# Hyena filter spectra from even and odd taps: half the transform matmuls on TensorE, sums and differences on VectorE

## What is computed

```
h = (sin-MLP of position features) -> (L, 2, n_ch); h = h * exp(-t * |deltas|)
h_full = concat([h[:, 0], zeros(1), h[1:, 1][::-1]]); h_full /= sum |h_full|
filt_f = rfft(h_full)                       # spectrum of each filter, for 2 orders
for n, gate in enumerate((x1, x2)):         # order o = 0, 1
    z = gate * (irfft(rfft(z, 2L) * filt_f[:, n])[:L] + bias[n] * z)
```

## Time and profile before

| | us |
|---|---|
| median of 3 runs (2746.61 to 2751.88) | 2748.93 |
| the profiled execution, whole | 2745.32 |
| its span in the trace | 2743.7 |
| PE busy | 2642.8 (96%) |
| DVE busy | 1875.4 (68%) |
| ACT busy | 1309.8 (48%) |

### The profile page before, as it was taken

One profiled execution on the slowest core, in us unless ns is written; L12 is line 12 of the kernel. 1 busy time (PEld: TensorE's weight loads), 2 busy tenths in 40 slices (PEclk: granted clock), 3 DMA queues, 4 the chain that ended last, 5 costly groups with the idle time before them and its releaser, 6 DMA issues.

```text
span 2743.7 us, 48997 instructions
## 1 busy us (share of the span) xinstructions
PE 2642.8 (96%) x17192; PEld 2341.7 (85%) x17192; DVE 1875.4 (68%) x3349; ACT 1309.8 (48%) x2366; POOL 111.9 (4%) x206
## 2 busy tenths in 40 slices
PE   7999999999999999999989999999999999999998
PEld 6889999888987778998779999988799877799986
DVE  7788787634567867566678778786255678765666
ACT  5555555534553333453455555555355433344535
POOL 2100000000000000000030000000000000000000
PEclk9999999999999999999999999999999999999999
DMA  7544444334453324555564444443444423345554
GB/s 244 163 151 154 150 144 154 130 138 140 147 170 100 116 100 148 182 176 173 165 197 155 152 145 149 151 151 119 145 147 140 162 96 121 99 162 179 177 174 146
DMA packets 115982, 412.24 MB, mean 150 GB/s; under 512 B 15460, under 2 KB 15514, under 8 KB 115584
## 3 DMA queue, kind: packets, MB, share of 16 engines
q1 hardware_dynamic: 107424, 391.17, 42.7%
q0 software_dynamic: 8416, 19.18, 2.2%
HBM read 403.99 MB, written 6.29 MB: 150 GB/s over the span
## 4 chain that ended last, share of the span: by engine, by line
PE 86%; DVE 7%; issue 3%; ACT 2%; DMA 1%; PEldq 0%; PEld 0%; DVEq 0%; POOL 0%; POOLq 0%; ACTq 0%
PE bank L1543 30%; PE bank L1571 19%; PE bank L1573 9%; PE bank L1917 6%; PE bank L1525 5%; PE bank L1661 2%; PE bank L1643 2%; PE bank L1624 2%; PE bank L1815 2%; DVE WL L388 1%; PE bank L1729 1%; PE bank L1838 1%; PE bank L1609 1%; PE bank L1753 1%; PE bank L1752 1%
## 5 line engine op out<-in xcount | busy, mean ns | idle before, releaser
L374 ACT ACTIVATE WH<-ring 128x512 fp32r<-128x512 f32 x1364 | 857.4, 631 | 1226.9 <-PE bank L1543 584.2
L388 DVE TENSOR_TENSOR WL<-ring,WH 128x512 fp32r<-128x512 f32 x852 | 575.9, 690 | 482.8 <-ACT WH L374 480.6
L1571 PE MATMUL bank<-XX,WH 128*128 128x512 f32 x2304 | 820.6, 399 | 29.8 <-DVE XX L557 15.6
L1543 PE MATMUL bank<-XX,WH 128*128 128x256 f32 x3712 | 684.7, 287 | 13.4 <-DVE WL L388 8.8
L1573 PE MATMUL bank<-XX,WL 128*128 128x256 f32 x2304 | 644.6, 280 | 0.0
L1543 PEld LDWEIGHTS bank<-XX,WH 128*128 128x128 f32 x3712 | 581.9, 193 | 32.2 <-issue 24.1
L1571 PEld LDWEIGHTS bank<-XX,WH 128*128 128x128 f32 x2304 | 435.3, 189 | 130.4 <-DVE XX L557 15.6
L1543 PE MATMUL bank<-XX,WL 128*128 128x256 f32 x1856 | 526.9, 284 | 0.0
L379 DVE TENSOR_TENSOR WL<-ring,WH 128x512 fp32r<-128x512 f32 x512 | 351.4, 689 | 136.5 <-ACT WH L374 132.6
L1573 PEld LDWEIGHTS bank<-XX,WL 128*128 128x128 f32 x2304 | 437.2, 190 | 0.0
L1543 PEld LDWEIGHTS bank<-XX,WL 128*128 128x128 f32 x1856 | 357.8, 193 | 0.0
(11 more groups left out here) (302 smaller groups left out, 3499.1 us busy)
## 6 DMA issues: line engine op xcount, KB each, us to landing
ring<-in_blocks SPq DMA_DIRECT2D x738, 512.0 KB, 3.3
ARENA<-in_bc POOLq DMA_DIRECT2D x2, 2048.0 KB, 9.9
ARENA<-in_decay POOLq DMA_DIRECT2D x8, 512.0 KB, 4.6
ARENA<-in_x SPq DMA_DIRECT2D x4, 512.0 KB, 9.0
u_scratch<-ARENA POOLq DMA_DIRECT2D x16, 128.0 KB, 2.3
ARENA<-u_scratch POOLq DMA_DIRECT2D x64, 32.0 KB, 3.2
y_scratch<-ARENA POOLq DMA_DIRECT2D x16, 128.0 KB, 2.0
ARENA<-y_scratch POOLq DMA_DIRECT2D x64, 32.0 KB, 2.8
```

Source lines behind the costliest of these rows:

```text
L374: nc.scalar.activation(wh[q], raw(which[0], q), ACT.Copy).then_inc(wh_ready[q], 1)
L388: vec.tensor_tensor(wl[q], raw(which[0], q), wh[q].bitcast(F32), ALU.subtract).then_inc(w_used[slot(which[0], half)], 1)
L1543: ins = mm(o, w_, x_, start=start and i == 0 and n == 0, stop=stop and i == 7 and n == 2)
L1571: ins = mm(bank[b][:, :], h, xx[:, :, k, :], start=(k == 0), stop=(k == DT - 1), skip_group_check=True)
```

## The change

The taps are held by time parity instead of by halves: the tap features, the decay table and the rows of `cos`/`sin` are reordered on the host, and `turn_z` transposes every second token of z instead of 128 neighbours. For the frequency 255 - f, the even taps give the same cosine sum as for f and the odd taps its negative (for the sine the signs are the other way round). So `filter_dft` makes four matmuls instead of eight: odd taps by cos and by sin to banks 4 and 5, even taps by cos and by sin to banks 6 and 7, each for 128 frequencies. ACT copies banks 4 and 5 alone. A new DVE function `unfold` makes the sum and the difference with banks 6 and 7 and writes both halves of `FRE` and `FIM`. It stands in the tail of steps 2 and 5, behind the last quarter of `WL` and ahead of the short convolution and `mix_in` there.

```
+                def unfold(o, c):
+                    for im, b in ((0, 6), (1, 7)):
+                        f = fit if im else frt
+                        even, odd = f[:, 0, c * CW:(c + 1) * CW], f[:, 1, c * CW:(c + 1) * CW]
+                        out_of(4 + im, "hyc", hyc(o, "dft", c, 4 + im))
+                        full(b, "hyc", hyc(o, "dft", c, b))
+                        st.did(v.tensor_tensor(even, bank[b][:, :], odd, ALU.add)); st.wait()
+                        if im:
+                            ins = v.tensor_tensor(odd, odd, bank[b][:, :], ALU.subtract)
+                        else:
+                            ins = v.tensor_tensor(odd, bank[b][:, :], odd, ALU.subtract)
+                        free(ins, b)
+                    out_of(6, "hyc", hyc(o, "dft", c, 6))
+                    out_of(7, "hyc", hyc(o, "dft", c, 7))
...
                         sums(o, s_ // 3)
+                    if s_ in (2, 5):
+                        unfold(o, s_ // 3)
...
                     if s_ in (2, 5):
                         c = s_ // 3
-                        for q in range(4):
-                            m, im = q // 2, q % 2
-                            full(4 + q, "hyc", hyc(o, "dft", c, 4 + q))
-                            dst = (FIM if im else FRE).rearrange("p (m c) -> p m c", m=2)[:, m, c * CW:(c + 1) * CW]
-                            free(a.activation(dst, bank[4 + q][:, :], ACT.Copy), 4 + q)
+                        for im in range(2):
+                            full(4 + im, "hyc", hyc(o, "dft", c, 4 + im))
+                            dst = (FIM if im else FRE).rearrange("p (m c) -> p m c", m=2)[:, 1, c * CW:(c + 1) * CW]
+                            free(a.activation(dst, bank[4 + im][:, :], ACT.Copy), 4 + im)
...
                     for q in range(4):
-                        m, im = q // 2, q % 2
+                        t, im = 1 - q // 2, q % 2
                         take_bank(4 + q, "hyc", hyc(o, "dft", c, 4 + q))
-                        for t in range(2):
-                            tab = (dft_sin if im else dft_cos)[:, t, m * P:(m + 1) * P]
-                            ins = mm(bank[4 + q][:, :], tab, ED[:, (im * 2 + t) * CW:(im * 2 + t + 1) * CW], start=(t == 0), stop=(t == 1))
-                            if t == 0:
-                                release(ins)
-                        done(ins, 4 + q)
+                        tab = (dft_sin if im else dft_cos)[:, t, 0:P]
+                        done(mm(bank[4 + q][:, :], tab, ED[:, (im * 2 + t) * CW:(im * 2 + t + 1) * CW], start=True, stop=True), 4 + q)
...
-                            ins = nc.tensor.transpose(bank[4 + q][:, j * P:(j + 1) * P], bct[:, half * 4 + j, t * P:(t + 1) * P], ident)
+                            ins = nc.tensor.transpose(bank[4 + q][:, j * P:(j + 1) * P], bct[:, half * 4 + j, t:T:2], ident)
```

More of the change, by code:

```diff
@@ L114 @@
 ZIN = 24 + WT
-DVE_STEPS, DVE_S5_STEPS = 450, 23
+DVE_STEPS, DVE_S5_STEPS = 458, 23
 SETUP_STEPS = 31
@@ L2037, in shape_constants @@
     ang = 2 * np.pi * (f + 0.5) * t / (2 * T)
-    fold = lambda a: a.reshape(2, P, T).transpose(1, 0, 2).reshape(P, 2 * T)
+    fold = lambda a: a[by_parity].reshape(2, P, T).transpose(1, 0, 2).reshape(P, 2 * T)
     order = np.concatenate([np.arange(P), 255 - np.arange(P)])
@@ L2058, in shape_constants @@
     decay = np.exp(-tl * np.abs(deltas)).astype(np.float32)
-    decay = decay.reshape(2, P, CHUNKS, CW).transpose(2, 1, 0, 3).reshape(CHUNKS, P, 2 * CW)
-    return con, angles, np.ascontiguousarray(feats.T), np.ascontiguousarray(decay)
+    decay = decay[by_parity].reshape(2, P, CHUNKS, CW).transpose(2, 1, 0, 3).reshape(CHUNKS, P, 2 * CW)
+    return con, angles, np.ascontiguousarray(feats[by_parity].T), np.ascontiguousarray(decay)
 def kernel(x, p, positions, w_in, s5_lambda_re, s5_lambda_im, s5_log_dt, s5_b_re, s5_b_im, s5_c_re, s5_c_im,
```

## The result

The changed kernel takes 2776.2 us (median of 4 runs, 2773.9 to 2778.0), the kernel before 2748.1 us (4 runs, 2746.6 to 2751.9). The ratio is 1.0104, with a 95% interval of 1.0092 to 1.0116: slower by 28 us. I had forecast slower by 10 us. The direction held, and so did the waits behind it; the size did not, because of the clock.

A forecast was written before the change was run, and what follows sets the result against it. PE was taken to bound the kernel (busy 96% of the span, 86% of the chain). Waits net of saved matmuls, +2.2 us, plus clock drops, +7.7, gave +9.9: from 2748.9 to 2758.8 us, range 2748 to 2766.

The forecast's parts named there:

- what bounds the kernel: Whole kernel: PE bounds it, busy 96% of the span and 86% of the chain, so matmul time removed should come back.
- what the matmuls are worth: At eight filter_dft places: half the matmuls go, 3.44 us at a place, 27.5 us in all.
- the added wait: In taps and turn_z: PE waits for banks 6 and 7, given back by DVE behind the last quarter of WL.
- the walk: Place-by-place account of a layer's four transforms, waits against saved matmuls: +1.1 us a layer, +2.2 us in two.
- the sums: In unfold: four added DVE operations a place, 32 in all, 22 us; bank 6 free 1.42 us after its start.
- the clock's term: At eight new PE idles in taps and turn_z: five clock drops of 1.54 us each, 7.7 us.
- My range: Whole kernel time: 8 in 10 range of 2748 to 2766 us.
- three drops: Lower edge of the forecast case of three to eight clock drops, 2753.5 to 2763.7 us; that case's chance 0.62.
- Strided loads: In turn_z, transposes loading every second token: bounds nothing to 2.8 us for four calls; taken as nothing.
- The banks come back in time: Rival at the take of bank 6 in taps and turn_z: full 27.5 us gain, 2721.4 us; chance 0.07.
- Few drops of the clock: Rival at the eight new PE idles: at most two clock drops, 2751.4 us; chance 0.24.

The follow-up runs named there:

- late unfold: Changed kernel with ACT copying all four banks and both unfold calls of an order moved to the tail of step 6: 2721.6 us, ratio 0.9899.
- the run that fills both idles: Changed kernel with extra matmuls, results overwritten, before the bank 6 waits: 22 in taps, 12 in turn_z: 2753.0 us, ratio 1.0012.
- the run with the clock held: Changed kernel with 22 extra matmuls, results overwritten, before the bank 6 wait in taps only: 2763.4 us, ratio 1.0057.
- the banks paired: Changed kernel with taps' first side-by-side pair dealt to banks 4 and 5, the second to 6 and 7: 2763.9 us, ratio 1.0055.

## Why the prediction was off, step by step

**Right: what bounds the kernel and what the matmuls are worth.** 3.44 us at a place, in the chain above to the digit, and 27 us in all once nothing waits (late unfold).

**Right: the added wait and its mechanism.** Banks 6 and 7 come back behind the last quarter of `WL`. The idle in `taps` was 2.64 us in order 0 and 2.40 us in order 1, against 2.8 and 2.35 of the walk. In `turn_z` it was 1.6 to 1.9 us for bank 6, against 2.2, and for bank 7 0.2 us in order 0 and 0.6 us in order 1, against 0.9. With the clock held, the first place lost 1.2 us against 1.1. The loop that makes the wait unavoidable stands in the chain of `turn_z`, order 0: PE's first transpose releases ACT's last quarter of `WH`, then comes DVE's `WL`, then `unfold`, and only then bank 6:

```profile
861.82 0.40 PE bank L1839
862.23 0.64 ACT WH L374
862.90 0.05 DVE WL L388
...
863.51 0.69 DVE ARENA L989
```

**Right: the sums.** 0.68 us for each operation, and bank 6 came back 1.41 us after `unfold` began (828.17 to 829.58), against 1.42. DVE's timeline in the changed kernel:

```profile
828.17 0.68 DVE L989 TENSOR_TENSOR ARENA<-bank,ARENA 128x512 f32<-128x512 f32 x1
828.89 0.69 DVE L993 TENSOR_TENSOR ARENA<-bank,ARENA 128x512 f32<-128x512 f32 x1
```

**Wrong: the size of the clock's term**, 5 x 1.54 = 7.7 us. It is 23 us by the run that fills both idles, 19 us of them seen at the eight places. The step failed in two places.

First, the count. I took a drop at five of eight places, and all eight had one in the profiled execution. The idles of `turn_z` stand close together, and I priced them as half a drop; without a drop the four places lose nothing (0.03 to 0.05 us each), with one 1.3 us each.

Second and larger, the price. I took 1.54 us from the earlier trace rows, a drop of some 3 us at half the clock. In step 2 of order 0 the low clock lasted 13.6 us and cost 5.7 us (6.9 less the 1.2 of the run with the clock held), in both layers. At the other six places a drop cost 1.3 us each, a little under my price. So three drops more than I took are worth 4.6 us at my price, the two long ones 8.3 us above it, and the other six together 1.5 us below it: 7.7 + 4.6 + 8.3 - 1.5 = 19.1 us.

Why the clock stayed low four times as long in order 0 is open. My price was read where full blocks follow, and here the rest of `taps` follows, single runs in half of the rows. That alone doesn't decide it, since the same matmuls follow in order 1, where the drop cost 1.3 us. The traces show one more difference: in order 0 the clock fell 1.3 us before PE went on, in order 1 about when PE went on. No run separates the two.

**My range** ended at 2766, since it allowed eight drops at that same price. The price had an uncertainty of its own, and I gave it none. Two sums under it are also off: few drops gives 2751.1 to 2754.2 us and not 2751.4 (2748.9 + 2.2 and up to 3.1), and three drops give 2755.7 us and not 2753.5 (2748.9 + 2.2 + 4.6).

**Strided loads.** My bounds were nothing and 2.8 us, and I took nothing; measured is 0.9 us.

**Rivals.** "The banks come back in time" gave 2721.4 us; the kernel in which they do measures 2721.6. That this is so near is partly luck, since executions of one kernel differ by several us. For the changed kernel itself the rival was rightly held unlikely. "Few drops of the clock" fell: all eight places had one.

## What to carry to other kernels

Before moving a PSUM read-out to another engine, look at what stands ahead of the reader on that engine, and whether any of it waits for what TensorE does next: then the bank can't be back when TensorE asks, as here with the last quarter of `WL`. Let the engine that was early go on reading, and do the arithmetic in SBUF where the other engine idles. Price an idle of TensorE with the clock that it may cost, and give that price a wide range: waits of 2.64 and 2.40 us, with the same matmuls behind them, cost 5.7 us and 1.3 us through the clock.

## What the runs showed of the hardware

Added matmuls whose results are never used made the kernel 23 us faster. They stood in eight waits of 1.6 to 2.6 us, and the granted clock stayed at 1.00 there. This is worth knowing as a probe: it tells a wait's own cost from the clock's.

A low spell's length isn't fixed. Idles of 2.6 us were followed by 13.6 us at 1.2 GHz in the changed kernel, and 7 us with the banks paired. In order 1, 2.4 us of idle were followed by about 3.4 us in the changed kernel, and by no drop with the banks paired. Half-used rows one at a time, with no idle of this length before them, left the clock at 1.00 for 8 us. What sets the length of a low spell stays open.

Weight loads of every second fp32 element took 209 ns in the median against 141 ns for contiguous ones in the trace before; 16 transposes took 0.22 us more, and not 16 x 68 ns = 1.1 us. The Trainium skill, page "SBUF — State Buffer", section "Door 1: The DMA port swizzle", would let a step of two floats be free; this run disagrees, by 68 ns a load, most of it hidden behind the transposes.
